# A chunked recurrence on TensorE: products between opposite partition halves, issued in turn with products within one half

## What is computed

```python
def step(state, inp):
    r_t, w_t, k_t, v_t, a_t, b_t = inp
    sa = jnp.einsum('bhvk,bhk->bhv', state, a_t)
    state = (state * w_t[:, :, None, :] + sa[..., None] * b_t[:, :, None, :]
             + v_t[..., None] * k_t[:, :, None, :])
    return state, jnp.einsum('bhvk,bhk->bhv', state, r_t)
```

## Time and profile before

| | us |
|---|---|
| median of 3 runs | 4639.51 |
| lowest to highest | 4636.82 to 4644.62 |
| profiled execution, its own time | 4639.49 |
| span in the trace | 4638.0 |
| TensorE busy | 4333.9 (93%) |
| recurrence, layer 0: 489.2 to 722.3 | 233.1 |
| recurrence, layer 1: 1881.6 to 2114.7 | 233.1 |

### The profile page before, as it was taken

One profiled execution on the slowest core, in us unless ns is written; L12 is line 12 of the kernel. 1 busy time (PEld: TensorE's weight loads), 2 busy tenths in 40 slices (PEclk: granted clock), 3 DMA queues, 4 the chain that ended last, 5 costly groups with the idle time before them and its releaser, 6 DMA issues.

```text
span 4638.0 us, 76648 instructions
## 1 busy us (share of the span) xinstructions
PE 4333.9 (93%) x33564; PEld 3399.0 (73%) x33564; DVE 1980.6 (43%) x2957; ACT 1528.6 (33%) x2699; POOL 571.7 (12%) x398
## 2 busy tenths in 40 slices
PE   7899999899998899899899998988899999899999
PEld 5676896677776676896677776765778888666877
DVE  4536434455434536434455434347432221443332
ACT  2533232333332533232333333237321121343221
POOL 1215100011002215101011001102000000150000
PEclk9999999999998999999999998999999999899999
DMA  4122101244422122101344421110011111101222
GB/s 147 42 96 72 35 4 60 96 150 167 155 82 101 42 100 73 35 4 60 105 150 164 156 85 41 51 37 1 32 51 64 63 60 60 54 10 55 96 88 90
DMA packets 97647, 351.90 MB, mean 76 GB/s; under 512 B 10017, under 2 KB 13601, under 8 KB 95905
## 3 DMA queue, kind: packets, MB, share of 16 engines
q1 hardware_dynamic: 86432, 313.02, 19.7%
q10 hardware_dynamic: 10880, 33.96, 2.0%
HBM read 332.26 MB, written 14.68 MB: 75 GB/s over the span
## 4 chain that ended last, share of the span: by engine, by line
PE 52%; DVE 4%; ACT 1%; POOL 1%; issue 1%; ACTq 0%; DVEq 0%
PE ps L341 13%; PE ps L342 13%; PE ps L344 13%; PE ps L1260 5%; PE ps L2233 1%; DVE sml L2308 1%; POOL e L2753 1%; PE ps L2668 1%; PE ps L2670 1%; DVE hm_lo L428 1%; PE ps L2669 1%; DVE hm L437 1%; PE ps L2255 1%; PE ps L2536 1%; PE ps L2122 1%
## 5 line engine op out<-in xcount | busy, mean ns | idle before, releaser
L302 DVE TENSOR_TENSOR wlo<-ring,whi 128x1024 fp32r<-128x1024 f32 x494 | 626.2, 1268 | 1911.4 <-ACT whi L292 1911.2
L292 ACT CAST whi<-ring 128x1024 fp32r<-128x1024 f32 x494 | 517.8, 1048 | 2210.8 <-PE ps L344 1916.6
L341 PE MATMUL ps<-h_hi,whi 128*128 128x512 f32 x1424 | 597.6, 420 | 33.1 <-DVE wlo L302 16.5
L342 PE MATMUL ps<-h_lo,whi 128*128 128x512 f32 x1424 | 568.9, 400 | 0.0
L344 PE MATMUL ps<-h_hi,wlo 128*128 128x512 f32 x1424 | 568.1, 399 | 0.0
L341 PE MATMUL ps<-hm_hi,whi 128*128 128x512 f32 (+1 forms) x1408 | 518.6, 368 | 21.3 <-DVE hm_lo L428 21.3
L342 PE MATMUL ps<-hm_lo,whi 128*128 128x512 f32 (+1 forms) x1408 | 483.3, 358 | 0.0
L344 PE MATMUL ps<-hm_hi,wlo 128*128 128x512 f32 (+1 forms) x1408 | 421.3, 357 | 0.0
L341 PEld LDWEIGHTS ps<-h_hi,whi 128*128 128x128 f32 x1424 | 272.6, 191 | 178.8 <-issue 73.0
L341 PEld LDWEIGHTS ps<-hm_hi,whi 128*128 128x128 f32 x1408 | 268.2, 190 | 98.0 <-issue 19.9
L341 PE MATMUL ps<-ac_hi,whi 128*128 128x512 f32 x880 | 330.8, 376 | 6.4 <-DVE ac L2448 6.4
(11 more groups left out here) (394 smaller groups left out, 7610.5 us busy)
## 6 DMA issues: line engine op xcount, KB each, us to landing
ring<-in_w SPq DMA_DIRECT2D x590, 512.0 KB, 3.4
h_spill<-h ACTq DMA_DIRECT2D x2, 2048.0 KB, 6.7
x_spill<-x ACTq DMA_DIRECT2D x2, 2048.0 KB, 14.9
m_spill<-m ACTq DMA_DIRECT2D x2, 2048.0 KB, 9.4
h_again<-h_spill ACTq DMA_DIRECT2D x2, 2048.0 KB, 8.0
ma<-m_spill ACTq DMA_DIRECT2D x2, 2048.0 KB, 10.0
x<-x_spill ACTq DMA_DIRECT2D x2, 2048.0 KB, 10.1
x<-in_x SPq DMA_DIRECT2D x1, 2048.0 KB, 10.8
```

Of the source, the lines that this page charges most:

```text
L292: self.A.copy(self.hi[k % 2][:], raw).then_inc(self.s_cut_hi.h, 1)
L302: self.V.tensor_tensor(self.lo[k % 2][:], raw, self.hi[k % 2][:].bitcast(F32), ALU.subtract).then_inc(self.s_cut_lo.h, 1)
L341: T.matmul(ps[:, b, 0:cw], hi, xh(q, c0, cw), start=q == 0, stop=False, skip_group_check=True)
L342: T.matmul(ps[:, b, 0:cw], hi, xl(q, c0, cw), start=False, stop=False, skip_group_check=True)
```

## The change

Tokens now stand on the half opposite to a head's channels. So a product whose rows are tokens and whose result has tokens ("tt"), or channels and channels ("dd"), stays on one half and uses the two quarters as before. A product from channels to tokens ("dt") or back ("td") goes from one half to the other, on the two other quarters. `scan_pe` has two programs per group, `scan_own` and `scan_across`, each with its own semaphore, and issues them in turn, two heads of one, then two heads of the other, as long as both have something in the place. There are eight places, not nine.

```diff
+        end = PLACES * (NCH + 1)
+        for k in range(end + LAG):
+            groups = [g for g in (1, 0) if 0 <= k - LAG * g < end]
+            a, b = (itertools.chain(*(place(program[g]) for g in groups)) for program in (own, across))
+            more = True
+            while more:
+                more = False
+                for side in (a, b):
+                    for _ in side:
+                        more = True
+                        break
...
+        def rows(kind, u):
+            return slice(64 * u, 64 * u + 64) if kind == "d" else slice(64 - 64 * u, 128 - 64 * u)
...
+        def product(way, bank, at, wide, *terms, begin=True, signal=None):
             for j in range(GP):
                 for u in range(2):
-                    rows = slice(64 * u, 64 * u + 64)
+                    src, dst = rows(way[0], u), rows(way[1], u)
```

```diff
+            if old:
+                act(c, "tb")
+                act(c, "u")
+                if new:
+                    act(c, "y8")
+                yield from product("td", 0, 0, CH, (mat("bkt", 0), mat("u")), (mat("bkt", 1), mat("vt")), signal=sx)
...
+            if old:
+                own(c, "u")
+                A.copy(m["u"][:, mine, :], one(1)).then_inc(sa, 1)
...
+        def with_rr(c, name):
+
+            own(c, name)
+            V.tensor_tensor(m["aa"][:, mine, :], one(1), m["rr"][:, mine, :], ALU.add).then_inc(sv, 1)
```

More of the change, by code:

```diff
@@ L1239, in woven, with scan_pe, place @@
             yield
-    def scan_pe(self, g, m, ops, base):
-        T, ps = self.T, self.ps
[L1243 to L1254, removed]
+    def scan_pe(self, m, ops, base):
+        own = [self.scan_own(g, m, ops, base[g]) for g in range(2)]
+        across = [self.scan_across(g, m, ops, base[g]) for g in range(2)]
+        def place(program):
+            for done in program:
+                if done:
+                    return
+                yield
+        end = PLACES * (NCH + 1)
[9 more added lines that the diff above has]
+                        break
@@ L1263, in product @@
-            return i
+                        i = T.matmul(ps[dst, 4 * g + bank, at + j * wide:at + (j + 1) * wide], lt(src, GP * g + j),
+                                     rh(src, GP * g + j), start=begin and j == 0 and n == 0,
+                                     stop=n == len(terms) - 1, skip_group_check=True)
+                if j == GP - 1 and signal:
+                    i.then_inc(signal, 1)
+                yield False
         def mat(name, part=None):
@@ L1330, in scan_pe @@
                 dve(c, "p3")
-                product(2, 0, CH, (Y, Pw)).then_inc(sp, 1)
+                yield from product("tt", 2, 0, CH, (Y, Pw), signal=sp)
             if old:
-                product(0, 0, CH, (mat("bkt", 0), mat("u")), (mat("bkt", 1), mat("vt"))).then_inc(sp, 1)
-            yield
+                dve(c, "a3")
+                yield from product("tt", 1, 0, CH, (mat("pf"), mat("aa")), signal=sp)
+            yield True
             if new:
                 dve(c, "p4")
[L1337 to L1341, removed]
@@ L1342, in scan_pe @@
-            yield
-            if new:
[L1344 to L1351, removed]
-            if new:
[L1353 to L1358, removed]
+                yield from product("tt", 3, 0, CH, (Pw, mat("ot")), signal=sp)
@@ L1376, in scan_act @@
             yield
-            if old:
-                pe(c, "rr")
-                A.copy(m["rr"][:, mine, :], one(1)).then_inc(sa, 1)
             yield
             if new:
-                pe(c, "tx")
+                own(c, "tx")
                 A.copy(m["zz"][:, mine, 0, :], one(2)).then_inc(sa, 1)
+            if old:
+                across(c, "rr")
+                A.copy(m["rr"][:, mine, :], one(1)).then_inc(sa, 1)
+                across(c, "tb")
+                A.copy(m["bkt"][:, mine, :, :], two(3)).then_inc(sa, 1)
             yield
             if new:
-                pe(c, "x2")
+                own(c, "x2")
                 A.wait_ge(self.s_sg2[g].h, base[3] + SCAN_POOL.after(c, "pw"))
@@ L1456, in scan_dve @@
             if new:
-                pe(c, "p3")
-                V.tensor_tensor(Pw, one(3), Pw, ALU.add).then_inc(sv, 1)
-            yield
-            if new:
-                pe(c, "p4")
-                V.tensor_tensor(Pw, one(2), Pw, ALU.add).then_inc(sv, 1)
+                own(c, "tp")
+                V.tensor_copy(m["pf"][:, mine, :], one(2)).then_inc(sv, 1)
             if old:
-                pe(c, "st")
+                across(c, "st")
+                own(c, "ya")
                 V.tensor_tensor(m["st"][:, mine, :], one(0), m["st"][:, mine, :], ALU.add).then_inc(sv, 1)
```

212 lines of the change are left out of this document (128 added, 84 removed).

## The result

The changed kernel takes 4618.1 us (median of 5; 4613.3 to 4620.8) against 4639.6 (4636.8 to 4645.3): ratio 0.9946, with an interval of 0.9934 to 0.9958. That is 21 us or half a per cent less. It is faster, but by a quarter of the 80.6 us forecast, and outside the range of 4510 to 4615. All ratios here are of fast runs alone; what they leave out is one run of the kernel before, at 10,810 us, among those of experiment 3.

The account below looks back on a forecast made before the run. TensorE's quarters were taken to bound the recurrence at 27.86 us per chunk. Work 19.5 plus waits 3.0 gave 22.5, with starts and ends 192.8 per layer against 233.1: 4639.5 - 80.6 = 4559 us, range 4510 to 4615.

Parts of the forecast that it names:

- What bounds the kernel before: In the recurrences, TensorE's array quarters set the 27.89 us chunk of both groups, not the issue of instructions.
- The sum that met the period: Per chunk, 2 x (208 x 0.0585 + 16 x 0.110) = 27.86 us of matmuls against a 27.89 us period, so nothing else counts.
- Can four quarters work at once: In the changed recurrence, own and across products run on all four quarters at full pace, though they share rows.
- the rival built on it: Quarters sharing rows don't work together in the recurrence: 29.9 us per chunk, 4673 us in all; 10%.
- TensorE's work after, 19.5 us: Recurrence slots A to D, each costed by its slower side: 9.74 us, twice per chunk, 19.5 against 27.86.
- The waits that appear, 3.0 us: TensorE's stalls per chunk of the recurrence for copies, adds and its own results: 3.0 us together, giving 22.5 per chunk.
- the starts and ends: Each layer's slots outside the seven full periods: 9.8, 7, 8.5 and 11 us, hand estimates good to 5 us.
- The issue-bound rival: In the recurrence, issuing records with their loads limits four quarters: 2.3 us more per chunk, 4594 us; 9%.
- The deeper-queue rival: Enough TensorE records wait ahead in the recurrence to shrink stalls: 19.5 us per chunk, 45 us less, 4514; 9%.
- The sign and the mechanism: Faster by over 0.2% at 84%, through four quarters overlapping in the recurrences, clock near 1, the rest unchanged.

Follow-up runs that it names:

- experiment 3: Each 128-column matmul of the recurrence issued as two of 64, in both kernels, against the kernel before: changed kernel 0.9996, kernel before 1.0016.
- ladder: Changed kernel plus stretches of independent matmuls alone ahead of layer 0's recurrence; 512 of 64 columns took 32.2 us on two quarters, 30.3 on four.

## Why the prediction was wrong

**What bounds the kernel before**: right, and incomplete. 27.86 us of quarters is the limit, but the supply of instructions stood only some 1.4 us below it (7.0 x 3.78 = 26.5), and its row was on the page that was read: 266 packets of instructions in 4638 us. The sum that met the period ruled supply out as the limit there, and said nothing of how near it was.

**Can four quarters work at once**: right. Four records per 58 ns in the changed kernel, 14.7 ns from one to the next in the ladder. The rule of the Trainium skill that a load overlaps matmuls only with another row group ("TensorE: Matmul & The Clock Gate", section "The mechanism") is against both traces, and the rival built on it fell: with the overlap taken away the ratio was 1.0011, with it 0.9946.

**TensorE's work after, 19.5 us**: right as work, 19.2 by the starts.

**The waits that appear, 3.0 us**: near in sum, 3.2, but in part by luck. By the starts `u` cost 1.2 us per chunk (foreseen 1.1), `mk` 1.0 (0.5), `x4` 0.6 (0.4) and `x2` 0.4 (0.4), together 3.2 against 2.4; the other 0.6, put down for `yy`, `rr` and `q`, shows as no wait of the middle.

**The step that failed** is the addition of the two to 22.5 us as if nothing else could bind. A third limit was missing: 6.75 packets at the ladder's 3.78 us are 25.5 us per chunk, and the means are 25.7 and 25.4. It came in as 3.0 us of stops per chunk. The two recurrences are 55 us longer than forecast. Group 0's first copy of `rr` and its eighth are seven periods apart, 174.9 us in layer 0 and 175.8 in layer 1, where 156.5 were forecast: that is 38 of the 55. The other 17 are in the starts and ends, 8.5 per layer, which were hand estimates called good to 5. Few stops on issue fall there, 1.1 us in layer 0 and 0.6 in layer 1, so the supply doesn't explain them; no run took them apart.

**The issue-bound rival** was the right kind of doubt at the wrong price. It had 9%, and 4594 us from a pace midway between two rows. The argument against it, 7.5 ns per load in the earlier trace rows, rested on a burst of eight; the other burst there, four loads started within 0.06 us, gives 20. A burst that short says nothing of the supply: within a packet the ladder shows 8 ns per instruction, and over its 2,048 instructions 14.8 (30.26 us). The one figure that came near the time, 4614 by the 25 ns from start to start of the Trainium skill ("TensorE: Matmul & The Clock Gate", section "Wait — 56ns, not 53.3ns?"), did so for another reason: in the ladder records do start 14.7 ns apart, 128 at a time.

The deeper-queue rival fell too: its sign was a period near 19.5 without idle time.

A rule that was not weighed bears on the failed step. The Trainium skill ("Runtime: NRT & Kernel Launch", section "Instruction fetch mechanics") says that instructions come in blocks of 16 KiB, which the packets here confirm, and that the cost of crossing a block is mostly hidden, since the sequencer issues more slowly than the blocks arrive. In the kernel before the trace agrees, with no stop in the middle. In the changed kernel it does not, with 3.0 us of stops per chunk: in the ladder the engine runs a block in 2.1 us and gets the next after 3.7 to 4.0.

**The sign and the mechanism** held: faster, by overlap in the recurrence alone, with the clock near 1. The size was cut to a quarter.

## What to carry to other kernels

Count the instructions of the busiest engine, not only its time: a matmul of float32 with its loads is four here, and 256 took some 3.8 us to arrive where nothing else bound (30.26 us for eight packets). Where an edit makes an engine denser, compare that supply (packets in a period x 3.7 to 3.8 us) with the work that would be left; the packets are on the page, and in the DMA view of any stretch, before anything is changed. Where supply is the slower of the two, a wait taken away buys less than its length (7 and 8 us of some 16 in the two pairs here), and a wider moving matrix with the same columns buys what its missing instructions are worth.

## What the runs showed of the hardware

- Instructions reach TensorE in packets of 16,384 bytes, 256 instructions. With nothing else to bind, TensorE began a new one every 3.73 or 4.00 us (`ladder`, a mean of 3.78); in the changed kernel single intervals go from 3.3 to 5.2, with the same mean of 3.78. In the ladder a packet starts 1.1 to 1.6 us after work on the one before has begun. All this is with little other DMA (4 GB/s); whether more of it slows the packets, no run tested.
- All four 64x64 quarters of the array take float32 records at once, own and crossing, with the same rows: 14.7 ns from start to start in the ladder, and four per 58 ns with different weights in the changed kernel.
- An instruction that only checks a value long reached is not free on TensorE: 109 ns each in a row of nothing else, 34 ns each for 1,600 of them in the changed kernel (54 us), 16 ns each for 1,536 in the kernel before (24 us).
